# Two engines' orders in a two-block transformer kernel: gates of the recurrent layer on ScalarE, softmax statistics on VectorE

## What is computed

```python
# recurrent layer (odd_mixer): 12 heads of 128
p = h @ w_in; xr, gate = split(p)
xc = causal_depthwise_conv(xr, conv_w, conv_b)          # 4 taps
r = sigmoid(xc_head @ w_rg + b_rg); i = sigmoid(xc_head @ w_ig + b_ig)
log_a = -8 * r * softplus(-lam); a = exp(log_a)
b = sqrt(-expm1(2 * log_a)) * (i * xc)
hs = scan(a, b)                                          # h_t = a_t h_(t-1) + b_t
y = hs * silu(gate) @ w_out
# state space: B's discrete form
bb_r = coef_r * b_re - coef_i * b_im; bb_i = coef_r * b_im + coef_i * b_re
# attention: 16 query heads, 4 key heads, blocks of 128, window of 128, with sinks
m = max(max(s), sink); pr = exp(s - m)
w = pr / (sum(pr) + exp(sink - m)); o = w @ v
```

## Time and profile before

| what | us |
|---|---|
| median of 3 runs | 1796.75 (1791.58 to 1796.85) |
| the profiled execution | 1796.26 |
| its span, first to last instruction | 1794.5 |
| TensorE (PE) busy | 1742.2 |
| GpSimd (POOL) busy | 986.4 |
| VectorE (DVE) busy | 903.3 |
| ScalarE (ACT) busy | 767.4 |

### The profile page before, as it was taken

The page is one execution under the profiler, slowest core; times in us unless marked ns, Lnnn a source line. Parts: engine busy times, 40 slices in busy tenths (PEclk is TensorE's granted clock), DMA queues, the critical chain, the costliest instruction groups (busy, mean ns, idle before and its releaser), DMA issues.

```text
span 1794.5 us, 20970 instructions
## 1 busy us (share of the span) xinstructions
PE 1742.2 (97%) x8022; PEld 1422.2 (79%) x8022; DVE 903.3 (50%) x1293; ACT 767.4 (43%) x1203; POOL 986.4 (55%) x614
## 2 busy tenths in 40 slices
PE   9999999999998889999999999999999999999998
PEld 7887888777787788888888888886557888888886
DVE  3999987666695784522211212646664221212124
ACT  5333335377756663343232323534555332323234
POOL 5859655676568365654444445655336444444464
PEclk9999999999998999999999999999999999999999
DMA  4222323222343134223222322221112232223221
GB/s 167 96 93 94 108 92 121 92 83 82 105 177 133 65 102 140 96 93 103 96 94 95 101 98 94 94 94 59 36 36 70 84 104 96 94 94 103 97 94 59
DMA packets 55540, 172.05 MB, mean 96 GB/s; under 512 B 6416, under 2 KB 14224, under 8 KB 54544
## 3 DMA queue, kind: packets, MB, share of 16 engines
q1 hardware_dynamic: 55440, 170.70, 28.0%
HBM read 164.65 MB, written 6.03 MB: 95 GB/s over the span
## 4 chain that ended last, share of the span: by engine, by line
PE 64%; DVE 7%; ACT 4%; issue 4%; POOL 3%; POOLq 0%; DVEq 0%; ACTq 0%
PE B L313 52%; PE B L2232 1%; POOL ACC L366 1%; PE B L2143 1%; PE B L296 1%; PE B L297 1%; PE B L298 1%; ACT WH L285 1%; PE B L1636 1%; DVE SW L1127 1%; PE B L2214 1%; DVE TMP L2166 1%; PE B L1386 1%; POOL WL L289 0%; PE B L1844 0%
## 5 line engine op out<-in xcount | busy, mean ns | idle before, releaser
L289 POOL TENSOR_TENSOR WL<-RAW,WH 128x1024 fp32r<-128x1024 f32 x281 | 682.4, 2431 | 602.0 <-ACT WH L285 601.9
L285 ACT ACTIVATE WH<-RAW 128x1024 fp32r<-128x1024 f32 x281 | 296.5, 1058 | 660.5 <-PE B L313 623.7
L313 PE MATMUL B<-P0h,WH 128*128 128x512 f32 x1104 | 433.5, 393 | 2.3 <-ACT WH L285 2.2
L313 PE MATMUL B<-P0l,WH 128*128 128x512 f32 x1104 | 426.0, 391 | 1.3 <-DVE P0l L430 1.3
L313 PE MATMUL B<-P0h,WL 128*128 128x512 f32 x1104 | 278.5, 389 | 1.9 <-POOL WL L289 1.9
L313 PEld LDWEIGHTS B<-P0h,WH 128*128 128x128 f32 x1104 | 207.9, 188 | 47.4 <-issue 3.3
L313 PEld LDWEIGHTS B<-P0l,WH 128*128 128x128 f32 x1104 | 207.9, 188 | 45.7 <-DVE P0l L430 2.3
L313 PEld LDWEIGHTS B<-P0h,WL 128*128 128x128 f32 x1104 | 207.2, 188 | 45.3 <-POOL WL L289 2.3
L437 DVE TENSOR_TENSOR H<-H,B 128x512 f32<-128x512 f32 x88 | 60.2, 686 | 281.0 <-PE B L313 281.0
L1913 DVE SCALAR_TENSOR_TENSOR TMP<-B,RS 128x512 f32<-128x512 f32 x64 | 44.1, 691 | 260.0 <-PE B L313 244.0
L313 PE MATMUL B<-P1h,WH 128*128 128x512 f32 x448 | 174.7, 390 | 0.0
(11 more groups left out here) (349 smaller groups left out, 2805.1 us busy)
## 6 DMA issues: line engine op xcount, KB each, us to landing
RAW<-in_w SPq DMA_DIRECT2D x281, 512.0 KB, 3.2
PX<-in_zeros SPq DMA_DIRECT2D x4, 1024.0 KB, 9.9
H<-in_xT SPq DMA_DIRECT2D x8, 256.0 KB, 5.3
g<-GB SPq DMA_DIRECT2D x8, 256.0 KB, 2.1
GB<-g SPq DMA_DIRECT2D x32, 64.0 KB, 2.0
out<-Q SPq DMA_DIRECT2D x4, 512.0 KB, 3.6
CA<-in_zeros SPq DMA_DIRECT2D x1, 1920.0 KB, 10.0
u<-TMP SPq DMA_DIRECT2D x7, 256.0 KB, 2.0
```

Of the source, the lines that this page charges most:

```text
L285: act.activation(WH[:, i % NS, :], RAW[:, i % NR, :], ACT.Copy).then_inc(*inc("w_hi", i))
L289: pool.tensor_tensor(WL[:, i % NS, :], RAW[:, i % NR, :], WH[:, i % NS, :].bitcast(F32), ALU.subtract).then_inc(*inc("w_lo", i))
L313: return pe.matmul(b[:, :], w[:, ws[c]], x[:, c, :], start=start, stop=stop)
```

## The change

Three things are reordered, and no arithmetic changes.

1. Recurrent layer. `worked(n)` and `parted(n)` become the same, the head of the stage before. ScalarE's first step of a head (tap 0 or Silu) is a function of its own, `act_first`. At the stage ahead of an R unit ScalarE does neither the weight copy nor the first step nor parts; they stand inside the R unit's stage: two heads' sigmoids, the parts of n - 2 of before (`act_parts(act, n - 1)`), tap 0 if that stage is an X unit, two heads' sigmoids, Silu if it is a G unit, weight copies of n + 2, the parts of the head just ahead, weight copies of n + 3, four Tanh. A one-element Sigmoid is also issued at G5. On VectorE, B's discrete form moves from G8 and G9 to R2, both parts at once.
2. Attention's VectorE order. Sum of n - 1 first, then the low part of the output of n - 3 (n - 2 before), both score reads of n, and then both maxima with the small operations.
3. GpSimd's splits of the `wob` units come after n = 0, 2, 4, 7 instead of 0, 2, 4, 6.

```diff
     def worked(n):
-        out = [n - 1] if kind_at(n) != "R" else []
-        if kind_at(n + 1) == "R":
-            out.append(n)
-        return [ODD[i] for i in out if kind_at(i) and kind_at(i) in "XG"]
-
-    def parted(n):
-        out = [n - 2, n - 1] if kind_at(n) == "R" else [n - 1] if kind_at(n + 1) != "R" else []
-        return [ODD[i] for i in out if kind_at(i) and kind_at(i) in "XG"]
+        return [ODD[n - 1]] if kind_at(n - 1) and kind_at(n - 1) in "XG" else []
+
+    parted = worked
...
             if kind == "R":
                 act_gates(act, pair(c, 0))
+                act_parts(act, n - 1)
+                if kind_at(n - 1) == "X":
+                    act_first(act, n - 1)
+                act_gates(act, pair(c, 1))
+                if kind_at(n - 1) == "G":
+                    act_first(act, n - 1)
+                highs(act, IDX[what] + 3)
                 act_parts(act, n)
-                act_gates(act, pair(c, 1))
-            highs(act, min(IDX[what] + 4, GLU0))
-            if kind == "X":
...
+                highs(act, IDX[what] + 4)
+            elif kind_at(n + 1) != "R":
+                highs(act, min(IDX[what] + 4, GLU0))
+                act_first(act, n)
             if kind == "R":
...
-            else:
+            elif kind_at(n + 1) != "R":
                 act_parts(act, n)
...
-            elif (kind, c) in (("X", 2), ("X", 9)):
+            elif (kind, c) in (("X", 2), ("X", 9), ("G", 5)):
                 act.activation(SM[:, 12 + c % 2:13 + c % 2], SM2[:, 0:1], ACT.Sigmoid)
+
+    def act_first(act, n):
+        kind, c = ODD[n]
+        if kind == "X":
+            if c == 1:
+                stat_copy(act, "odd")
+            for h in xs_of(c):
+                act.wait_ge(*at("xp", h))
+                w = VE[:, VCOL["conv_c_w"] + 4 * h:VCOL["conv_c_w"] + 4 * h + 1]
+                act.activation(own_bank("X", h), XP[:, h % 2, 0:T], ACT.Identity, bias=vec("conv_c_b", h),
+                               scale=w).then_inc(*inc("xc0", h))
+        elif kind == "G":
+            act.wait_ge(*at("g_x", c))
+            act.activation(own_bank("G", c), own_bank("G", c), ACT.Silu).then_inc(*inc("g_silu", c))
...
-            if kind == "G" and c in (8, 9):
-                dve_b(dve, c - 8)
+            if (kind, c) == ("R", 2):
+                dve_b(dve, 0)
+                dve_b(dve, 1)
...
-        dve.wait_ge(*at("att_s", ("s", n, hp)))
-        dve.tensor_reduce(st[:, 2 * hp:2 * hp + 2], sv, AX.X, ALU.max).then_inc(*inc("att_d", (n, "max", hp)))
-        if hp == 0:
-            return
+
+    def dve_maxima(dve, n):
+        kv = place(n)[0]
+        st = AS[:, n, :]
+        for hp in range(2):
+            dve.wait_ge(*at("att_s", ("s", n, hp)))
+            dve.tensor_reduce(st[:, 2 * hp:2 * hp + 2], s_view(n, hp), AX.X, ALU.max).then_inc(
+                *inc("att_d", (n, "max", hp)))
...
         for n in range(18):
+            if 0 < n < 17:
+                dve_sum(dve, n - 1)
+            if n > 2:
+                dve_out(dve, n - 3)
             if n < 16:
                 dve_scores(dve, n, 0)
-            if 0 < n < 17:
-                dve_sum(dve, n - 1)
-            if n < 16:
                 dve_scores(dve, n, 1)
+                dve_maxima(dve, n)
...
-            if n > 1:
-                dve_out(dve, n - 2)
             if n == 2:
                 dve_p(dve, 1)
+        dve_out(dve, 15)
...
-            if n % 2 == 0:
+            if n in (0, 2, 4, 7):
                 lows(pool, IDX[("wob", 0, n // 2)] + 4)
```

More of the change, by code:

```diff
@@ L905, in act_odd @@
                 act_gates(act, pair(c, 0))
-                act_parts(act, n)
-                act_gates(act, pair(c, 1))
-            highs(act, min(IDX[what] + 4, GLU0))
-            if kind == "X":
[L910 to L919, removed]
+                act_parts(act, n - 1)
[5 more added lines that the diff above has]
+                highs(act, IDX[what] + 3)
+                act_parts(act, n)
+                highs(act, IDX[what] + 4)
+            elif kind_at(n + 1) != "R":
+                highs(act, min(IDX[what] + 4, GLU0))
+                act_first(act, n)
             if kind == "R":
@@ L2158, in dve_scores @@
         kv, blk, k0, nk, p_ = place(n)
-        st = AS[:, n, :]
         sv = s_view(n, hp)
```

## The result

The changed kernel takes 1780.15 us (median of 4 runs, 1777.45 to 1781.62) beside 1795.46 for the kernel before in the same series (4 runs, 1791.58 to 1796.85): a ratio of 0.9916, 95% interval 0.9895 to 0.9938. That is 15.3 us faster, more than the 0.3% that can be told from no change. In the ratios of this document one execution of the kernel before, at 3129.43 us and a mean granted clock of 0.724 in a later series, is left out. The profiled execution took 1779.3, its span is 1777.5, against 1796.26 and 1794.5: 17.0 less.

The account below looks back on a forecast made before the run. TensorE was taken as the bound, busy 1742.2 of 1794.5 us, leaving 52 us to win by reordering. Layer 5, attention 7 and MLP's start 3 sum to 15, taking 1796.26 to 1781 us, range 1774 to 1791.

Parts of the forecast that it names:

- R0, nothing: Recurrent layer's first gate unit: 0.9 us left from earlier sigmoids, given back at X11; 0, bounds 0 and -0.9.
- R1, -1.5: Second gate unit: first sigmoid at 414.8 instead of 416.24, so 1.5 us less, with about 1.5 idle in the middle.
- R2, 3.7 earlier: Third gate unit: gate at 455.8 instead of 458.99; TensorE leaves 3.7 us earlier, R1's 1.5 included.
- B, cost 0, and 0.3 for the bank at G10: B's six VectorE operations fit R2's tail, ending by 471 to 474.6, at no cost; G6's bank frees 0.3 late for G10.
- O0's add 6.0 earlier, the layer 5: After the layer: O0's add comes 6.0 us earlier; the chain to the square sums gives the layer 5, bounds 1 and 7.5.
- Attention, -7: Attention loop: idle 7.0 becomes 2.6 and 2.6 of the clock's 4.0 goes; -7 us, bounds -11 and +6.
- MLP's start, -3: MLP's start: swapping GpSimd's last split removes the 1.39 us wait and 1.7 of clock; -3, bounds -1.4 and -3.3.
- The two waits that were to remain: Attention: TensorE idle of 0.9 us at n = 3 and 1.65 after n = 8 and 9 was expected to remain.
- (a): Rival, chance 0.24: attention gives nothing because the longer loop eats what the score reads give; 1788 us.
- (b): Rival, chance 0.13: the layer gives 1 because table switch and queue delay exp(8), stopping TensorE for 4; 1785 us.
- (c): Rival, chance 0.09: layer and attention both fall short, or the entry's chain starts no earlier; only MLP's start counts, 1793.
- (d): Rival, chance 0.04: slower, since GpSimd's split holds VectorE's small operations in attention; three more such cases give 1805 us.

Follow-up runs that it names:

- attention alone: The kernel before with only attention's new VectorE order; 1787.79 us, ratio 0.9945 to before.
- the layer alone: The kernel before with only the recurrent layer's edits (sigmoid order, early table load, B's discrete form at R2); 1792.74 us, ratio 0.9968 to before.

## Why the prediction was right, and where it wasn't

The forecast was 1781 (1774 to 1791), the result 1780.15. All three edits gained, and at the places that were named. That the sum of 15 came out so closely is in part luck: over several traces the layer gives 7.5 where 5 was said and attention 5.4 where 7 was said, and the two errors go against each other. By its own steps:

- **R0, nothing.** Right: TensorE has 0.46 of idle for VectorE's split at X11 (row of 406.43), the give-back that was named.
- **R1, -1.5.** Its first gate is at 414.29 where 414.8 was said. The way was another, though: the unit's waits are 1.6 and 1.5, nearly the one of 3.3 before, and what made it 1.6 shorter is the low stretch of 1.7 us at 417, which is gone. It stands in all four traces with the old gates and in none of the ten with the new. The prediction read an idle of 1.5 for two splits in the middle of this unit before; that trace has none there, the stretch lies over it.
- **R2, 3.7 earlier.** Its last matmul ends 4.4 earlier (461.06, before 465.46); gate at 455.02 (455.8 said). The step "the load moves into ScalarE's wait (a one-element Sigmoid at G5)" had the wrong cause: without that Sigmoid the load is as early.
- **B, cost 0, and 0.3 for the bank at G10.** The step that failed. "End by 471 to 474.6; exp comes near 475.4": B ended at 475.28 and exp's product could have started near 474.1 (475.77 with the offset, in the kernel with B in halves). The sum took 7.6 for the locks from two stages; here, beside GpSimd's weight splits, it was 9.5. TensorE paid 1.33 at G10, which the prediction itself had named as a sign that it would be wrong. Done in halves this price goes.
- **O0's add 6.0 earlier, the layer 5.** 5.3 and 4.7 at the square sums. That chain, not TensorE, set the time: the wait stayed, at 4.38, not 3, since chain and TensorE moved together. What was left out is the clock between the square sums and attention: the layer gave 6.8 by the first scores in the profiled pair, and 7.5 over several traces.
- **Attention, -7.** 7.2 in the profiled pair, 5.4 against the mean of four old-order traces. The size rested on the worst wait of the earlier trace rows, and the other old-order traces have no such wait: one execution's case was read as the rule. In the prediction's terms, the idle of 7.0 is 5.8 on the mean and becomes 2.6 as said, and the clock gives 1.1 instead of 2.6. The two waits that were to remain, 0.9 at n = 3 and 1.65 with the lock, came at 1.56 and 1.00, with the causes named; of the first the 3.33 of idle in front was not seen.
- **MLP's start, -3.** 1.4 of wait and 1.6 of clock: 3.0.

The rivals: (a) falls by attention alone (ratio 0.9945), (b) by the layer alone, (c) by both. (d), the lock: it is there. The row of 1246.26 ends at 1247.54. Below stand GpSimd's split beside it, a second pair, and the pair that TensorE pays for:

```profile
1245.18 2.35 POOL L289 TENSOR_TENSOR WL<-RAW,WH 128x1024 fp32r<-128x1024 f32 x1
...
1269.12 1.27 POOL L2102 TENSOR_TENSOR RP<-RP,RO 128x512 f32<-128x512 f32 x1 [4.56 <-PE B L2090]
1269.13 1.28 DVE L2186 TENSOR_SCALAR AS<-AS 128x4 f32<-128x4 f32 x1
...
1296.28 2.38 POOL L289 TENSOR_TENSOR WL<-RAW,WH 128x1024 fp32r<-128x1024 f32 x1 [0.79 <-ACT WH L285]
1297.02 1.65 DVE L2184 TENSOR_TENSOR AS<-AS,VE 128x4 f32<-128x4 f32 x1
```

The first ends at 1247.53, the last two at 1298.66 and 1298.67. That agrees with the Trainium skill (SBUF — State Buffer, Who interferes with whom), by which a VectorE operation with two inputs in SBUF contends with a GpSimd operation that reads SBUF. The middle pair has one tensor input on VectorE and is held too, as is one more like it at 1235.65. In all, after has five small operations of over 1 us in attention, the longest 1.65, where before had four, the longest 2.43. The one of 1297.02 costs TensorE 1.00: the exponentials start at 1298.97, the sum at 1301.18, the score reads at 1302.27, and the scores that wait for them at 1303.00.

## What to carry to other kernels

Where two engines are nearly level on the path, an edit for one of them shows little (1.1 and 2.0 alone, 4.7 together): look for what the other waits for before dropping it. Work that fills an engine's gap should be priced with what its neighbours do in that gap: the same three operations took 2.0 us in one idle and 5.4 in another. And a wait's size should be read in more than one execution, if there are any, before it goes into a sum.

## What was not expected of the hardware

**A table load doesn't wait for its function's data.** It ran at 452.93, 2.2 us ahead of the sigmoid that it is for. The Trainium skill (ScalarE: Activation LUTs, What ACT_TABLE_LOAD costs) gives 2.66 with a drain; here the load is 1.28, and the rest isn't seen.

**The clock falls or doesn't after the same idle.** TensorE waits 1.9 us for GpSimd ahead of 172.57 in the kernel after and in the one with later weight splits. The four us behind that wait, by stretch, in after:

```profile
173.00:177.00 4.00, 4.00 (x19) 3.28 (x18) 4.00 (x7) 1.67 (x2) 4.00 (x3) 1.00 0.41 131
```

and in the other, where nothing differs up to there:

```profile
173.00:177.00 4.00, 4.00 (x12) 3.10 (x11) 4.00 (x7) 1.65 (x2) 4.00 (x3) 0.57 0.42 131
```

12 matmuls instead of 19: the same idle costs 1.7 us more in one execution than in another, and of the 14 traces, which all have it (1.88 to 1.93), 7 show the stretch. What decides it stays open. Idles that were shortened or removed took stretches with them: that at 417 (four of four traces before, none of ten behind the change), and that at the MLP's start (three of four, none of ten). So one trace may show such a stretch or not, and several have to be read.
